# A two-block transformer kernel on one core: two paired units and fourteen column sums rewritten

## The reference

```python
# first block: 3 x 2048 values; only the gate third matters here
shift, scale, gate = jnp.split(silu_c @ w_ada[l] + b_ada[l], 3, axis=-1)
...
# second block: 6 x 2048 values
mod = c_act @ w_mod[l] + b_mod[l]
shift1, scale1, gate1, shift2, scale2, gate2 = [t[:, None, :] for t in jnp.split(mod, 6, axis=-1)]
...
merged = (jax.nn.sigmoid(gate_a) * (o_a @ p_a[l]) + jax.nn.sigmoid(gate_b) * (o_b @ p_b[l]))
h = h + gate1 * (merged @ w_out[l])          # the second output projection
u = _rms(h, norm2_w[l]) * (1.0 + scale2) + shift2
ff = jax.nn.silu(u @ w_gate[l]) * (u @ w_up[l])
h = h + gate2 * (ff @ w_down[l])
```

## Time and profile before

| | |
|---|---|
| median of 3 runs | 2793.52 us (2793.42 to 2794.45) |
| profiled execution, its own time | 2793.06 us |
| span of its instructions | 2791.3 us |
| TensorE busy | 2767.6 us, 99% |
| VectorE busy | 2092.3 us, 75% |
| ScalarE busy | 1484.4 us, 53% |
| GpSimd busy | 344.3 us, 12% |
| mean granted TensorE clock | 0.998 of 2.4 GHz |

### The profile page before, as it was taken

How to read it: one execution, slowest core, us unless ns; L and a number is a source line. 1 busy time by engine, 2 the same in 40 slices (tenths; PEclk the granted TensorE clock), 3 DMA queues, 4 the chain that set the end, 5 groups by cost and what they waited for, 6 DMA issues and landing times. The chain is left out here.

```text
span 2791.3 us, 43493 instructions
## 1 busy us (share of the span) xinstructions
PE 2767.6 (99%) x16296; PEld 2396.5 (86%) x16296; DVE 2092.3 (75%) x3615; ACT 1484.4 (53%) x2430; POOL 344.3 (12%) x1005
## 2 busy tenths in 40 slices
PE   8999999999999999999999999999999999999999
PEld 4778888888888888888888888888888888888888
DVE  3478877888988887787887877878988765566654
ACT  3365454555666566666666644545554543444443
POOL 0023300000002343323242310000000000000000
PEclk9999999999999999999999999999999999999999
DMA  8966668888865555554555588788768756655554
GB/s 324 350 226 211 206 199 274 285 266 298 299 177 198 179 171 171 168 189 160 185 177 173 176 268 283 253 291 296 253 211 284 251 179 191 194 190 186 187 184 148
DMA packets 182899, 621.85 MB, mean 223 GB/s; under 512 B 20240, under 2 KB 28704, under 8 KB 181920
## 3 DMA queue, kind: packets, MB, share of 16 engines
q1 hardware_dynamic: 182688, 619.08, 66.4%
HBM read 612.69 MB, written 4.21 MB: 221 GB/s over the span
## 5 line engine op out<-in xcount | busy, mean ns | idle before, releaser
L271 PE MATMUL ps<-act,whi 128*128 128x512 f32 (+1 forms) x6560 | 1757.1, 398 | 4.1 <-DVE act L266 2.2
L256 DVE TENSOR_TENSOR wlo<-raw,whi 128x1024 fp32r<-128x1024 f32 (+3 forms) x883 | 1044.6, 1188 | 429.2 <-ACT whi L247 232.5
L271 PEld LDWEIGHTS ps<-act,whi 128*128 128x128 f32 (+1 forms) x6560 | 1165.7, 189 | 213.4 <-issue 14.5
L271 PE MATMUL ps<-act,wlo 128*128 128x256 f32 (+2 forms) x6416 | 990.8, 287 | 0.3 <-DVE wlo L256 0.3
L247 ACT ACTIVATE whi<-raw 128x1024 fp32r<-128x1024 f32 (+3 forms) x883 | 880.7, 1024 | 181.9 <-PE ps L271 149.8
L271 PEld LDWEIGHTS ps<-act,wlo 128*128 128x128 f32 (+1 forms) x6416 | 895.0, 190 | 66.4 <-issue 1.7
L247 ACT ACTIVATE t<-ps 128x256 f32<-128x256 f32 (+2 forms) x400 | 149.9, 376 | 456.0 <-PE ps L271 417.8
L266 DVE SCALAR_TENSOR_TENSOR acc<-raw,c_act,acc 128x1024 f32<-128x1024 f32 x210 | 267.7, 1277 | 0.0
L262 POOL TENSOR_SCALAR small<-small 128x2 f32<-128x2 f32 (+3 forms) x256 | 92.3, 361 | 974.3 <-DVE small L262 954.5
L256 POOL TENSOR_TENSOR small<-small 128x2 f32<-128x2 f32 (+2 forms) x460 | 170.8, 371 | 258.0 <-ACT t L247 172.4
L247 ACT ACTIVATE t<-t 128x256 f32<-128x256 f32 (+3 forms) x248 | 108.0, 438 | 174.9 <-DVE t L256 150.3
(11 more groups left out here) (224 smaller groups left out, 1970.6 us busy)
## 6 DMA issues: line engine op xcount, KB each, us to landing
raw<-in_w SPq DMA_DIRECT2D x418, 512.0 KB, 5.0
raw<-in_w_mod SPq DMA_DIRECT2D x192, 512.0 KB, 4.7
raw<-in_w_gate SPq DMA_DIRECT2D x88, 512.0 KB, 4.4
raw<-in_w_up SPq DMA_DIRECT2D x88, 512.0 KB, 4.5
raw<-in_w_s SPq DMA_DIRECT2D x64, 512.0 KB, 7.1
raw<-in_w_out SPq DMA_DIRECT2D x64, 512.0 KB, 5.6
raw<-in_w_down SPq DMA_DIRECT2D x64, 448.0 KB, 3.6
raw<-in_w_ada SPq DMA_DIRECT2D x32, 512.0 KB, 5.2
```

What stands on the lines that cost most here:

```text
L256: return (q or DV).put(lambda e: e.tensor_tensor(o, a, b, op), needs, cost=max(0.4, size(o) * 0.0036) if q else 0.07 + size(o) * 0.00104)
L271: return PE.put(lambda e: e.matmul(o, w, x, start=start, stop=stop), needs, tell, cost)
```

## The change

The first two units of the second output projection share their items by `together`, four items of kind B in place of four of kind G, and `ms` is called after each with half the rate. The other fourteen units stay. The column sums are no longer split into high and low part. `m_sum` runs four native fp32 matmuls with 32 columns of ones as weights, each over 256 columns of the accumulator (eight pieces of 32 at a stride of 128), into its own 32 partitions of one bank. Partition 32q + i then holds the sum of column 128j + 32q + i for each j. `m_keep` takes it out with eight products of 32 columns with a tiled 32x32 identity, which is added to the constants `COLS`. It waits for TensorE by `hop` before it is queued, and takes a tile of 256 columns (`t1`) where it took one of 512 (`t2`). The accumulator is released by the matmuls, where it was by the subtraction.

```diff
--- before.py
+++ after.py
@@ -34,7 +34,8 @@
 
 C_C, C_CC, C_C2, C_BADA, C_NG, C_FG, C_BMOD, C_N1, C_N2 = 0, 16, 32, 48, 96, 112, 128, 224, 240
 C_QG, C_KG, C_QN, C_KN, C_ON, C_EPS, C_E2, C_SEL, C_CONV = 256, 257, 258, 259, 260, 261, 262, 264, 272
-N_COLS = C_CONV + 192
+C_E32 = C_CONV + 192
+N_COLS = C_E32 + 32
 
 M_SX, M_AX, M_SC, M_AC, M_GATE, M_MOD, M_A1, M_A2, M_ON, M_FG = 0, 1, 2, 3, 4, 5, 11, 12, 13, 14
 
@@ -483,17 +484,6 @@
                 t = stt(a, raw, w, a, ALU.mult, ALU.add, it["in"] + state[key])
             state[key] = t
             raw_free[it["raw"]] = t
-        elif kind == "F":
-            n = ring["hi"]
-            ring["hi"] += 1
-            it["n"] = n
-            hi, lo = HI[n % NH], LO[n % NL]
-            key = ("acc", it["half"])
-            a = ACC[:, 1024 * it["half"]:1024 * it["half"] + 1024]
-            t = copy(hi[:, :], a, state[key] + pe_free["hi", n - NH])
-            u = lo_part(lo[:, :], a, hi[:, :], t + pe_free["lo", n - NL])
-            it["hi"], it["lo"] = t, u
-            state[key] = t + u
 
     state = {"start": True}
 
@@ -1161,30 +1151,25 @@
     def m_sum(it):
 
 
-        n = it["n"]
-        b = []
-        for c in range(2):
-            bank, f = grab_bank()
-            w = slice(512 * c, 512 * c + 512)
-            mm(bank[:, :], ONER[:, :], HI[n % NH][:, w], True, False, f + it["hi"] + state["one_r"])
-            t = mm(bank[:, :], ONER[:, :], LO[n % NL][:, w], False, True, it["lo"], tell=True)
-            b.append((bank, t))
-        pe_free["hi", n] = pe_free["lo", n] = t
-        start(m_keep(it["slot"], 8 * it["half"], it["bias"], b))
-
-    def m_keep(slot, at, bias, b):
-        d, f = yield from t2.take()
-        for c in range(2):
-            bank, t = b[c]
-            done = []
-            for j in range(4):
-                i = at + 4 * c + j
-                done += stt(d[:, 128 * j:128 * j + 128], bank[:, 128 * j:128 * j + 128], 1.0, ident, ALU.mult, ALU.mult,
-                            t + f + state["k1"], accum=MOD[:, slot, i:i + 1])
-            banks.give(bank, done)
-            f = done
-            yield None
-        t2.give(d, done)
+        key = ("acc", it["half"])
+        a = ACC[:, 1024 * it["half"]:1024 * it["half"] + 1024].rearrange("p (j q i) -> p j q i", q=4, i=32)
+        bank, f = grab_bank()
+        PE.wait(f + state[key])
+        for q in range(4):
+            o = bank[32 * q:32 * q + 32, 0:256].rearrange("p (j i) -> p j i", i=32)
+            t = mm(o, ones[:, 0:32], a[:, :, q, :], True, True, tell=q == 3, cost=0.11)
+        state[key] = t
+        start(m_keep(it["slot"], 8 * it["half"], it["bias"], bank, t))
+
+    def m_keep(slot, at, bias, bank, t):
+        d, f = yield from t1.take()
+        yield from hop(t + f)
+        done = []
+        for j in range(8):
+            done += stt(d[:, 32 * j:32 * j + 32], bank[:, 32 * j:32 * j + 32], 1.0, col(C_E32, 32), ALU.mult, ALU.mult,
+                        t + f, accum=MOD[:, slot, at + j:at + j + 1])
+        banks.give(bank, done)
+        t1.give(d, done)
         o = MOD[:, slot, at:at + 8]
         state["sec", slot] = state.get(("sec", slot), []) + tt(o, o, col(bias + at, 8), ALU.add, done)
         state["halves", slot] = state.get(("halves", slot), 0) + 1
@@ -2042,7 +2027,12 @@
 
     add({"kind": "X", "run": last_b})
     add({"kind": "X", "run": ln_table})
-    for n in range(16):
+    first = together([(256, rhs_m2, lambda b, t, n=n: start(out2_job(n, b, t))) for n in range(2)],
+                     lambda i, m, w: src["w_out2"][0:2, :, w].rearrange("u p c -> p u c"))
+    for x in first:
+        stream.extend(x)
+        ms(R_FF / 2)
+    for n in range(2, 16):
         gemm(f"out2_{n}", tile_o("w_out2")(n), HALVES, rhs_m2, lambda b, t, n=n: start(out2_job(n, b, t)))
         ms(R_FF)
     tile_d = lambda n, half: lambda k, p: src["w_down"][n, :, 128 * (22 * half + k):128 * (22 * half + k + p)]
@@ -2189,6 +2179,7 @@
     put(C_CONV, x["conv_w_2"][0].reshape(4, 48, 128).transpose(2, 1, 0).reshape(128, 192))
     for q in range(4):
         cols[32 * q:32 * q + 2, C_SEL:C_SEL + 2] = np.eye(2)
+    cols[:, C_E32:C_E32 + 32] = np.tile(np.eye(32), (4, 1))
     cols[:, C_EPS], cols[:, C_E2] = EPS, EPS * EPS
     d["cols"] = cols
     d["k1"], d["k2"] = _constants()
```

## The result

The changed kernel takes 2788.32 us (median of 19 runs, 2785.05 to 2789.68), the kernel before 2793.21 us on the same chips (19 runs, 2790.68 to 2796.11). The ratio is 0.9982, with a 95% interval of 0.9975 to 0.9988: 4.9 us less, where 4.3 were forecast. The forecast of 2789.2 us lies 0.9 above the measured time. The gain of 0.18% is under the 0.2% that I had set as the bound. It is so close to it that the interval reaches over it (0.25% to 0.12%).

The account below looks back on a forecast made before the run. TensorE, busy 99% of the span, was taken to bound the kernel. -2.43 + 0.15 - 2.1 + 0.05 = -4.3 us from 2793.06 gives 2788.7, as a median 2789.2; range 2786.6 to 2792.2.

Parts of the forecast that it names:

- the 0.2% that I had set as the bound: Whole kernel: a difference under 0.2% (5.6 us) counts as none; faster is under 2787.9 us, slower over 2799.1.
- What bounds: Whole kernel: TensorE is busy 99% of the span; only matmul time taken out and the one stop count.
- The pairing: Second output projection: the stop at operand 15 goes, -2.43 us; four items alternating high and low parts cost +0.15.
- The cover: Second output projection: operand 15 is ready 2.9 us before its matmul; even 2.2 us more delay leaves 0.8.
- The column sums: Fourteen sums on TensorE: each takes 0.76 us against 0.91, switching in and out included; -2.1 us in all.
- Rival A: Job order shifts with the sums' new clock entries; idle before 1936 us changes by up to 3.0 either way; chance 0.20.
- the 1 us that I had set as its sign: TensorE idle between 186 and 1936 us differing from 3.0 us by more than one would show the order shifted.
- Rival B: Second output projection: the stop moves; operand 15 or a weight low part is late by up to 2.43 us; chance 0.10.
- C: Column sums: entry and exit are free, each sum 0.44 us, saving 6.6 us, total 2784.7; chance 0.05.
- D: Column sums: the narrow matmuls do not overlap, 2.08 us each, +14.2 us, total 2807.7; chance 0.05.
- The 0.05 us for the larger constants load: Kernel start: constants grow by 128 bytes a partition, 16 KB at 329 GB/s, +0.05 us.

Follow-up runs that it names:

- The crossed items: Changed kernel with both halves' column sums in one entry and the first two output-projection units crossed as ordinary items, not shared: 2785.19 us, ratio 0.9975.
- it with the line moved: Kernel before with only ScalarE's 1.28 us table load put four units later in the second output projection: 2790.01 us in one execution.

## Why the prediction was right

**What bounds.** Right. The whole gain is found in TensorE's starts: less work in the sums, the stop, and less idle time elsewhere.

**The pairing, forecast -2.43 + 0.15.** The stop went, as forecast. The paired items cost nothing extra: 0.347 us a pair in the changed kernel, not the 0.3535 of the feed forward, 11.1 us for four items against 11.2 in the old order. The low part's wait of 0.23 us was missing from the sum. By the starts (projection to next sum) the kernel with both parts takes 28.29 us against 30.35, of which 0.09 more is the entry of the new sum: 2.15 us, where 2.28 were forecast. Two errors of about 0.2 us nearly cancelled.

**The cover, forecast 2.9 us.** This step was wrong without a consequence. I allowed for pb15's step moving back by one copy and one low part, 2.2 us at most, which would have left 0.8. The operand was 2.7 us later from the projection's start, since an accumulation and a further low part came in behind `merge_a`, and the cover was 0.4. The crossed items, with 2.3 us less of cover, show that this is real: they stop for 1.6 us.

**The column sums, forecast 0.15 us each.** Right in mechanism and nearly in size: 0.57 us, 0.09 in and 0.10 out, in thirteen runs of records (two sums lie side by side and share one switch, which the forecast had not seen). On different groups of columns they overlap, as the two kernels with four more matmuls show. The strided moving operand costs nothing: 0.57 us here as in the start, where it is contiguous. By the distance between items it is 0.12 to 0.15 us each, 1.7 to 2.1 in all, and the shared switch gives 0.3 more. The Trainium skill ("TensorEngine Tiling (Array Packing)", Key Properties) says that a change of tiling mode drains TensorE. The rows agree, with 0.09 us in and 0.10 out. The type of the operands changes at the same two places, from fp32r to native fp32 and back, and no run separates the two.

**Rival A, the order.** It came in part, and on the side of a gain, by a little less than the 1 us that I had set as its sign. The idle time before 1936 us is 3.0 to 3.2 us in five profiled executions with the old sums. With the new sums it is 2.1 us in three, and 2.8 in a fourth, which has one more wait for a weight's low part, 0.70 us at 702. In the two kernels with four more matmuls a sum it is 1.6, and in the three with merged sums 1.0. **Rival B** did not come, with 0.4 us to spare at operand 15. **C** and **D** are out: no free switch, and no lack of overlap.

**The sum.** Starts of records give -2.15, -2.0 and -0.9, 5.1 us, against 4.9 in the medians, with an interval of 3.4 to 7.0. Runs of one kernel differ by more than 4 us, so the medians alone could not have told the parts apart. Much of that difference lies ahead of the first column sum, which starts between 391.97 and 396.21 in five executions whose program is the same up to there. From the first to the last of the column sums TensorE takes 1821.42, 1821.63 and 1821.70 us in three executions of the kernel before and 1816.34 and 1816.16 in two of the changed one, again 5.1 to 5.5 less.

That the forecast came so near is in part luck. The 0.9 us of idle time and the 0.3 of the shared switch stood in no term of it, and the separate sums gave up to 0.4 less than the 2.1 forecast. The 0.05 us for the larger constants load lies in the start, whose executions differ by 4 us, and no run shows it.

## What to carry to other kernels

Where one engine is full, price an edit in start-to-start distances on that engine, and count the way in and out of a changed array layout: here 0.33 us a time, twice what a sum saved, so that putting two halves into one switch gave nearly as much again as the new sums. An operand that is late at the start of a stage can be met by giving the engine more work that does not need it. But the cover must be worked out from the queue of the engine that makes the operand, with all that is put in between its steps. The chain of waits can pass through an instruction (here the table load) whose moving gives nothing. And where single executions differ by more than the change is worth, compare stretches of the trace between two marks that both kernels have.

## What the hardware showed that I had not expected

A granted clock of 0.57 over the 4 us behind a stop of 2.2 us, in one execution of six, at about 1.6 us. And the lower level is there early on too, in every execution whose windows I read, with a mean over the same 14 us of 0.63 in some and 0.76 in others. Kernels with the same start have either. What this costs is not shown: the first column sum starts at 395.57 us with 0.63 and at 391.97 with 0.76 in the old form, but at 395.01 with 0.63 (the column sums alone) and 396.08 with 0.76 (the changed kernel) in the new. The windows of the kernel before, of it with the line moved, and of the changed kernel:

```profile
31.00:45.00 14.00, 12.17 (x77) 7.45 (x81) 7.27 (x19) 5.34 (x9) 0.00 (x0) 0.63 0.88 353
```
```profile
31.00:45.00 14.00, 12.24 (x92) 7.75 (x85) 6.21 (x15) 4.29 (x7) 0.00 (x0) 0.76 0.82 315
```
```profile
31.00:45.00 14.00, 10.50 (x53) 6.77 (x57) 7.64 (x22) 5.34 (x9) 0.00 (x0) 0.76 0.92 364
```
